# Gate products of a recurrent layer as 64-row tiles, one per head, with dense gate weights and half-partition evictions

## The reference, cut to what matters

```
def block_diag_linear(u, w, b):
    y = jnp.einsum('bnhd,hde->bnhe', u.reshape(bsz, n, LRU_HEADS, LRU_BLOCK), w)
    return y.reshape(bsz, n, LRU_WIDTH) + b

def rglru_coeffs(u, w_a, b_a, w_x, b_x, lam):
    r = jax.nn.sigmoid(block_diag_linear(uf, w_a, b_a))
    i = jax.nn.sigmoid(block_diag_linear(uf, w_x, b_x))
    log_a = -LRU_C * r * jax.nn.softplus(-lam)
    a = jnp.exp(log_a)
    bterm = jnp.sqrt(-jnp.expm1(2.0 * log_a)) * (i * uf)
    return a, bterm
```

## Time and profile before

| | |
|---|---|
| median of 3 runs | 1627.05 us (1625.73 to 1629.73) |
| span of the profiled execution | 1627.5 us |
| PE, ACT, DVE, POOL busy | 1471.1, 745.3, 764.3, 587.3 us |
| layer 0's eight iterations | about 104 to 737 us |
| one iteration, from u_raw's read at 339.6 to the next one's at 418.68 | 79.08 us |

### The profile page before, as it was taken

One profiled execution on the slowest core, in us unless ns is written; L12 is line 12 of the kernel. 1 busy time (PEld: TensorE's weight loads), 2 busy tenths in 40 slices (PEclk: granted clock), 3 DMA queues, 4 the chain that ended last, 5 costly groups with the idle time before them and its releaser, 6 DMA issues. The chain is left out here.

```text
span 1627.5 us, 20425 instructions
## 1 busy us (share of the span) xinstructions
PE 1471.1 (90%) x7428; PEld 1185.9 (73%) x7428; DVE 764.3 (47%) x1063; ACT 745.3 (46%) x1190; POOL 587.3 (36%) x271
## 2 busy tenths in 40 slices
PE   7679999999999999976899994989999799999697
PEld 2268787878878787864688883878887678887476
DVE  1576464645554546455211123312222688887632
ACT  3537273736464545545122222222222688888421
POOL 0142322222222322304334342524443466666342
PEclk9899999999999999997899997999999799999799
DMA  7610303030303121108333434544432723222584
GB/s 288 232 64 13 115 14 114 13 114 13 114 17 111 36 92 56 59 33 286 96 113 105 127 104 153 146 116 129 129 117 89 217 92 112 82 97 66 152 231 134
DMA packets 93313, 178.73 MB, mean 110 GB/s; under 512 B 10390, under 2 KB 57270, under 8 KB 91082
## 3 DMA queue, kind: packets, MB, share of 16 engines
q1 hardware_dynamic: 93260, 178.04, 33.7%
HBM read 122.92 MB, written 45.13 MB: 103 GB/s over the span
## 5 line engine op out<-in xcount | busy, mean ns | idle before, releaser
L706 PE MATMUL slab<-h_hi,w_hi 128*128 128x512 f32 (+1 forms) x768 | 277.1, 361 | 19.1 <-POOL h_lo L699 16.9
L707 PE MATMUL slab<-h_lo,w_hi 128*128 128x512 f32 (+1 forms) x768 | 275.2, 358 | 0.0
L708 PE MATMUL slab<-h_hi,w_lo 128*128 128x512 f32 (+1 forms) x768 | 275.2, 358 | 0.0
L678 POOL TENSOR_TENSOR w_lo<-wraw,w_hi 128x1024 fp32r<-128x1024 f32 x32 | 87.2, 2726 | 452.7 <-ACT w_hi L419 452.7
L706 PEld LDWEIGHTS slab<-h_hi,w_hi 128*128 128x128 f32 x768 | 145.2, 189 | 48.0 <-issue 16.4
L707 PEld LDWEIGHTS slab<-h_lo,w_hi 128*128 128x128 f32 x768 | 145.1, 189 | 23.0
L708 PEld LDWEIGHTS slab<-h_hi,w_lo 128*128 128x128 f32 x768 | 145.2, 189 | 22.9
L1700 POOL TENSOR_TENSOR probs<-probs,rdenom 128x2560 f32<-128x2560 f32 (+1 forms) x32 | 135.8, 4242 | 58.4 <-DVE rdenom L1660 58.4
L1415 PE MATMUL slab<-h_hi,w_hi 128*128 128x512 f32 (+1 forms) x352 | 136.2, 387 | 16.6 <-DVE h_lo L1337 15.9
L1143 PE MATMUL Y<-wo_hi,m_hi 128*128 128x512 f32 x320 | 128.2, 401 | 25.0 <-DVE wo_lo L1041 23.4
L1416 PE MATMUL slab<-h_lo,w_hi 128*128 128x512 f32 (+1 forms) x352 | 135.6, 385 | 0.0
(11 more groups left out here) (251 smaller groups left out, 3009.7 us busy)
## 6 DMA issues: line engine op xcount, KB each, us to landing
wraw<-in_w_in SPq DMA_DIRECT2D x32, 512.0 KB, 3.9
wm<-in_wm SPq DMA_DIRECT2D x8, 1536.0 KB, 6.6
wm<-in_wm SPq DMA_DIRECT2D x16, 768.0 KB, 4.5
xt<-in_x SPq DMA_DIRECT2D x20, 512.0 KB, 6.5
mixT<-work SPq DMA_DIRECT2D x16, 640.0 KB, 5.4
mraw<-mixT SPq DMA_DIRECT2D x20, 512.0 KB, 5.1
q_parts<-qT SPq DMA_DIRECT2D x32, 256.0 KB, 4.3
oT<-o_out SPq DMA_DIRECT2D x8, 1024.0 KB, 3.8
```

Of the source, the lines that this page charges most:

```text
L706: nc.tensor.matmul(out, l_hi, r_hi, start=start, stop=False)
L707: nc.tensor.matmul(out, l_hi, r_lo, start=False, stop=False)
L708: return nc.tensor.matmul(out, l_lo, r_hi, start=False, stop=stop)
```

## The change

A gate unit is now a chunk with both gates: the weights of a head are a dense tile of 64 rows by 128 columns, 64 for gate a and 64 for gate x. Each head is one matmul that contracts over the 64 partitions of its channels and writes 128 partitions by n columns into a bank of its own. So a direction has three units of six matmuls (three precision terms by two heads) in place of six units of three matmuls; the number of matmuls, 18, and the columns of each stay. In the bank of head 0 gate a lies on partitions 0 to 63 and gate x on 64 to 127; head 1 has its columns swapped on the host, so that its x comes first.

ACT reads a unit with four Tanh instructions of 64 partitions, one per gate and head, where it had two of 128. Two of the four move the data to the other half of the partitions. Twelve instructions per direction stand where six stood, with the same columns. L440 now waits for all twelve. A unit takes two of the four banks of `W`, so that a unit waits for the reads of the unit two before it.

The gate weights shrink from 128x512 to 128x256 in SBUF, one DMA of 128 rows of 1 KB takes the place of two of 64 rows, and the memset of the zeros goes.

```diff
-        gw = sb("gw", [P, 4, P])
+        gw = sb("gw", [P, 4, HEAD])
...
-                for c in range(2):
-                    sp.dma_start(gw[HEAD * c:HEAD * (c + 1), :, HEAD * c:HEAD * (c + 1)],
-                                 a["w_gate"][t, HEAD * c:HEAD * (c + 1), :, :]).then_inc(gw_ld, 16)
+                sp.dma_start(gw[:], a["w_gate"][t]).then_inc(gw_ld, 16)
...
             def gates(t, d, first):
-                for x in range(2):
-                    dst = (A, B)[x]
-                    if x == 0:
-                        if d == 1:
-                            act.wait_ge(hd, 2 * t + 1)
-                        elif not first:
-                            act.wait_ge(mr, t)
-                    for c, (at, n) in enumerate(CHUNKS):
-                        k = 6 * d + 3 * x + c
-                        act.wait_ge(gp_, 12 * t + k + 1)
-                        nc.scalar.activation(dst[:, at:at + n], W[:, k % 4, 0:n], ACT.Tanh, scale=0.5,
-                                             bias=cur[:, C_HALF + 2 * x + d:C_HALF + 2 * x + d + 1]).then_inc(gr, 1)
-                act.wait_ge(gr, 12 * t + 6 * d + 3)
+                if d == 1:
+                    act.wait_ge(hd, 2 * t + 1)
+                elif not first:
+                    act.wait_ge(mr, t)
+                for c, (at, n) in enumerate(CHUNKS):
+                    p = 3 * d + c
+                    act.wait_ge(gp_, 6 * t + p + 1)
+                    for x in range(2):
+                        for head in range(2):
+                            src = HEAD * (x ^ head)
+                            nc.scalar.activation((A, B)[x][HEAD * head:HEAD * head + HEAD, at:at + n],
+                                                 W[src:src + HEAD, 2 * (p % 2) + head, 0:n], ACT.Tanh, scale=0.5,
+                                                 bias=cur[HEAD * head:HEAD * head + HEAD, C_HALF + 2 * x + d:C_HALF + 2 * x + d + 1])\
+                                .then_inc(gr, 1)
+                act.wait_ge(gr, 24 * t + 12 * d + 12)
...
-            nc.vector.memset(gw[:], 0.0).then_inc(zero, 1)
...
             def gate_products(t, d):
-                for x in range(2):
-                    for c, (at, n) in enumerate(CHUNKS):
-                        k = 6 * d + 3 * x + c
-                        if k < 3:
-                            pe.wait_ge(xr, 3 * t + k + 1)
-                        elif k > 3:
-                            pe.wait_ge(gr, 12 * t + k - 3)
-                        mm3(W[:, k % 4, 0:n], gw_hi[:, 2 * d + x, :], gw_lo[:, 2 * d + x, :],
-                            u_hi[:, at:at + n], u_lo[:, at:at + n], True, True).then_inc(gp_, 1)
+                for c, (at, n) in enumerate(CHUNKS):
+                    p = 3 * d + c
+                    if p < 2:
+                        pe.wait_ge(xr, 3 * t + 2 + p)
+                    else:
+                        pe.wait_ge(gr, 24 * t + 4 * p - 4)
+                    for g, v, start, stop in ((gw_hi, u_hi, True, False), (gw_hi, u_lo, False, False),
+                                              (gw_lo, u_hi, False, True)):
+                        for head in range(2):
+                            rows = slice(HEAD * head, HEAD * head + HEAD)
+                            last = nc.tensor.matmul(W[:, 2 * (p % 2) + head, 0:n], g[rows, 2 * d:2 * d + 2, :],
+                                                    v[rows, at:at + n], start=start, stop=stop)
+                    last.then_inc(gp_, 1)
...
             def dft_product(t):
-                pe.wait_ge(gr, 12 * t + 12)
+                pe.wait_ge(gr, 24 * t + 24)
```

More of the change, by code:

```diff
@@ L301, in mixers @@
         cur = sb("cur", [P, ALL_COLS])
-        gw = sb("gw", [P, 4, P])
-        gw_hi, gw_lo = sb("gw_hi", [P, 4, P], F32R), sb("gw_lo", [P, 4, P], F32R)
+        gw = sb("gw", [P, 4, HEAD])
+        gw_hi, gw_lo = sb("gw_hi", [P, 4, HEAD], F32R), sb("gw_lo", [P, 4, HEAD], F32R)
         A, B, C, H, sgf, fT, xf, u = (work[:, i, :] for i in range(KT))
@@ L383, in body @@
                 if first:
-                    sp.wait_ge(zero, 2)
+                    sp.wait_ge(zero, 1)
                 else:
                     sp.wait_ge(gwl, t)
-                for c in range(2):
-                    sp.dma_start(gw[HEAD * c:HEAD * (c + 1), :, HEAD * c:HEAD * (c + 1)],
-                                 a["w_gate"][t, HEAD * c:HEAD * (c + 1), :, :]).then_inc(gw_ld, 16)
+                sp.dma_start(gw[:], a["w_gate"][t]).then_inc(gw_ld, 16)
                 if not first:
@@ L462, in body @@
                 if first:
-                    act.wait_ge(zero, 2)
+                    act.wait_ge(zero, 1)
                 else:
@@ L479, in body @@
                 split_hi(t, SLAB_GF)
-                act.wait_ge(gw_ld, 32 * t + 32)
+                act.wait_ge(gw_ld, 16 * t + 16)
                 if not first:
-                    act.wait_ge(gp_, 12 * t)
+                    act.wait_ge(gp_, 6 * t)
                 nc.scalar.activation(gw_hi[:], gw[:], ACT.Copy).then_inc(gwh, 1)
@@ L611, in direction @@
                 def direction(d):
-                    dve.wait_ge(gr, 12 * t + 6 * d + 6)
+                    dve.wait_ge(gr, 24 * t + 12 * d + 12)
                     stt(out=B[:], in0=B[:], scalar=1.0, in1=u[:], op0=ALU.add, op1=ALU.mult).then_inc(iu, 1)
@@ L2081 @@
     w0 = slabs(g["l0_w_in"])
-    w_gate = np.stack([g["l0_w_a"][0], g["l0_w_x"][0], g["l0_w_a"][1], g["l0_w_x"][1]])
+    w_gate = np.stack([g["l0_w_a"][0], g["l0_w_x"][0], g["l0_w_a"][1], g["l0_w_x"][1]]).reshape(4, KT, 2, HEAD, HEAD)
     w1, kv = g["l1_w_in"], N_KV * HEAD
@@ L2098 @@
         "w_in0": np.stack([w0[0:8], w0[16:24], w0[24:32], w0[8:16]], 1).reshape(4 * KT, P, D),
-        "w_gate": w_gate.reshape(4, KT, 2 * HEAD, HEAD).transpose(1, 2, 0, 3),
+        "w_gate": np.stack([w_gate[:, :, 0], w_gate[[1, 0, 3, 2], :, 1]], 2).transpose(1, 2, 3, 0, 4).reshape(KT, P, 4, HEAD),
         "w_f": g["l0_w_f"],
```

## The result

The changed kernel takes 1715.05 us (median of 4, 1712.24 to 1716.13) against 1626.39 for the one before. The ratio is 1.0539, 95% interval 1.0523 to 1.0555: 5.4% slower. The direction was forecast, the size was not: 1699 was the value and 1712 the end of the range. The profiled execution has a span of 1714.4 us, 86.9 more than before.

The account below looks back on a forecast made before the run. The prediction took a chain of ACT reads, ACT passes, root and DVE scan up to the DFT product as the bound at the gates, PE elsewhere. 1627.5 + 51.0 (reads) + 20.6 (clock) - 0.4 (memset) = 1698.7, say 1699 us; range 1677 to 1712.

Parts of the forecast that it names:

- The bound: At the gates PE waits for ACT's reads, so PE's saving, at most half of 3.59 us per direction, counts nothing.
- The price of one read: ACT's gate reads: time goes by columns alone, so a read of 64 partitions costs the full price.
- rival 3: ACT's reads: price goes by partitions, twelve half reads take 3.01 us like six whole ones; 1630 us; chance 0.02.
- six more cost 3.01 us more: Direction 1's reads: six took 3.01 us, so twelve start the DFT product another 3.01 us later.
- twelve reads, 6.02 us: Direction 0's reads: no longer paced by PE, from 362.74 to 368.76; with the other terms L440 starts 3.35 us later.
- The start of direction 0: PE's first gate unit needs two banks free, so it starts after L495's second read, +0.42 us.
- the stretch to the scan's end: From L440 to the forward scan's end ACT and DVE have no slack, so the scan ends 3.35 us late.
- The gap before L440: L440 now waits for its direct predecessor: 0.14 us of lost overlap and a gap of 0.17 us as before L476.
- The change of array shape: PE switching tile shape before the first unit: taken as 0, bounds 0 and 8 x 0.33 = 2.6 us.
- The clock: PE's rests before the DFT product drop it to half clock, costing 2.6 us per iteration, 20.6 us in all.
- The rival without it: First rival: PE's clock holds through the rests before the DFT product; 1678 us; chance 0.10.
- The memset: Its removal ends PE's first-iteration wait for the ACT read behind it, gaining 0.4 us, between 0 and 0.42.

Follow-up runs that it names:

- e_whole: The changed kernel, but ACT reads each bank once over 128 partitions, six reads per direction, gates mixed up in the output; 1649.32 us, 1.0136 to the kernel before.
- e_low: The changed kernel, but from the second iteration on all reads read and write partitions 0 to 63, output wrong; 1696.35 us, 1.0407.
- e_twice: The kernel before with each gate read issued twice over 128 partitions, twelve whole reads per direction; 1691.67 us, 1.0382.
- e_halves: The kernel before with each gate read made as two reads of 64 partitions, low and high half, products unchanged; 1711.61 us, 1.0513.
- e_order: The changed kernel with a unit's four reads reordered by head, so the half written changes three times per direction, not eleven; 1709.44 us, 1.0497.
- e_whole_fill: e_whole with 14 idle matmuls before the third unit of direction 1 and 9 before the DFT product; 1629.65 us, 1.0016 to the kernel before.
- e_fill: The changed kernel with 46 idle matmuls before the third unit of direction 1 and 28 before the DFT product; 1703.08 us, 1.0459.
- e_root: The kernel before with direction 0's square root moved on ACT to right behind its gates, ahead of the split of slab G's weights; 1640.68 us, 1.0084.
- e_whole_root: e_whole with direction 0's square root right behind its gates and POOL's two passes held until the forward scan ends; 1624.53 us, 0.9979 to the kernel before.

## Why the forecast went wrong

The direction, the place and the order of the terms held. Point by point:

- The bound: PE waits for ACT's reads, so PE's saving counts for nothing. Right; the pairs run side by side as assumed, and the saving came back as rest. e_whole showed that it can be worse than nothing, since the rest lowered the clock.
- The price of one read: 682 and 469 ns, for 692 and 478 with 128 partitions. Right, and rival 3 (price by partitions) is out.
- **The step that failed** is the next one: "six more cost 3.01 us more", and "twelve reads, 6.02 us" in direction 0. I took the pace of reads that overlap their neighbours for reads that alternate between the halves. The true figure is 7.6 us per direction, 1.43 more than assumed in direction 1 and 1.31 in direction 0. Over eight iterations that is 22 us, and it puts the time outside the range. The prediction priced L476's gap behind its predecessor and the overlap at L440, but took the overlap inside the pace as given, with no bound for its loss. e_low and e_twice, at 1696 and 1692 us, are the forecast's sum as kernels; e_halves, e_low and e_order together show what takes the overlap away, up to the bias noted at e_order. Why a change of the half does it, the runs don't show.
- The start of direction 0 (+0.42, measured 0.47) and the stretch to the scan's end (no slack, measured 0.01) were right. The gap before L440 was not a term of its own: L440 starts 0.03 us after the last read has ended (404.56 for 396.92 + 7.61), where 0.31 was added for it.
- The change of array shape at nothing: right. The 2 us that e_whole_fill leaves are no more than the later first unit.
- The clock: 20.6 us forecast, 18 by the periods, 12 by e_fill, in which one iteration still paid 1.2 us for a fall. The mechanism was right and the size a little too large. The rival without it is out.
- The memset, at 0.4 us: no run has this change alone, but the trace of the changed kernel agrees. From the small product of the first iteration to slab F's first product it is 2.69 us (105.39 to 108.08) for 3.19 before (104.15 to 107.34), and the wait of 0.42 us is gone.

The Trainium skill (ScalarE: Activation LUTs, What ACT_TABLE_LOAD costs) gives the overlap of back-to-back ACTIVATEs as about 93 ns. The rows of e_low agree nearly, with 0.11 us (a length of 0.68 and a start 0.57 us on). Where the half changes the measurement decides: the reads of e_order start 0.71 us apart, without overlap. For e_root the Trainium skill (SBUF — State Buffer, SBUF: two separate sides) says that a DVE operation with two SBUF inputs and a GpSimd operation that reads SBUF share a port pair, that the one which starts first holds it for its whole instruction, and that the other is blocked until then. The trace of e_root agrees. POOL's two passes end at 382.10 and 385.38; scans that begin at 379.96 and 382.68, wait for these ends and then take their old 0.69 and 2.35 us would last 2.83 and 5.05 us, and 2.68 and 4.85 are measured.

## What to carry to other kernels

Count what a narrower or finer product does to the engine that empties it: twice the instructions at full price, plus the overlap with the neighbour for each that reads or writes other partitions than the one before. When a group's pace is taken from a trace, put a bound on what that pace contains. And an engine that waits gains nothing from shorter work; if it is PE, the rest can cost clock, so look for the clock over what comes right behind the wait.

## What the runs showed of the hardware

- ACT instructions over 128 or over 64 partitions, from PSUM, overlap by about 0.1 us with the next (e_low, e_twice). A change of the half read, or of the half written together with the half of the bias, takes that away: 0.71 for 0.58 us from start to start at 512 columns (e_order).
- Two fp32r matmuls over 64 rows each, in the two halves of the array and into two banks, take the time of one: pairs start 0.23 us apart at 512 columns (the changed kernel).
- Behind waits of 2.10 and 1.26 us with 0.6 us of work between, the clock had fallen in each of the seven iterations of e_whole that have them, and idle matmuls in them took 20 us off the program. Behind waits of 0.72 and 1.26 us it had fallen in four of eight (e_whole_root).
- A DVE scan of 2.35 us takes 4.85 us beside POOL's subtractions over SBUF (e_root).
